# A retention layer's streamed weights: the second pair of a head's accumulating DMAs waits for the DMA transposes of the gated values

## The reference

```python
q, k, v, g = split(rms_norm(h) @ w_in)             # 8 heads: q, k 256 wide; v, g 512 wide
scores = einsum('bnihd,bnjhd->bnhij', rot(q), rot(k)) * decay
y = scores @ v  (+ the state that the first chunk hands to the second)
y = normalise each head of y
h = h + (silu(g) * y) @ w_out                      # the gated values
h = h + sigmoid(rms_norm(h) @ w_gate) * (p @ w_proj)
```

## Time and profile before

| | us |
|---|---|
| median of 3 executions | 1563.88 |
| lowest and highest of the 3 | 1559.8, 1565.68 |
| the profiled execution, its own time | 1568.04 |
| its span, first to last instruction | 1566.0 |
| TensorE busy | 1531.3 (98% of the span) |
| VectorE, ScalarE, GpSimd busy | 1124.6, 926.2, 28.8 |
| mean granted TensorE clock | 0.994 of full |

### The profile page before, as it was taken

One profiled execution on the slowest core, in us unless ns is written; L12 is line 12 of the kernel. 1 busy time (PEld: TensorE's weight loads), 2 busy tenths in 40 slices (PEclk: granted clock), 3 DMA queues, 4 the chain that ended last, 5 costly groups with the idle time before them and its releaser, 6 DMA issues.

```text
span 1566.0 us, 19940 instructions
## 1 busy us (share of the span) xinstructions
PE 1531.3 (98%) x6788; PEld 1261.6 (81%) x6788; DVE 1124.6 (72%) x1390; ACT 926.2 (59%) x1108; POOL 28.8 (2%) x40
## 2 busy tenths in 40 slices
PE   9988989999999999999999999999999999999997
PEld 7777868888788888888888888888888888888885
DVE  6968768797888888787767585685577557756665
ACT  7447554664747475575767656644664466446853
POOL 0000000000000000000000000000000000000000
PEclk9999999999999999999999999999999999999999
DMA  9496695977768596976565666755665576555651
GB/s 385 155 217 232 204 190 177 281 222 207 227 211 236 188 264 201 266 223 215 181 225 192 205 225 188 243 204 199 196 233 191 195 228 212 218 191 198 215 192 78
DMA packets 137529, 333.11 MB, mean 213 GB/s; under 512 B 80992, under 2 KB 81008, under 8 KB 116368
## 3 DMA queue, kind: packets, MB, share of 16 engines
q1 hardware_dynamic: 132608, 314.35, 60.5%
q0 software_dynamic: 4736, 17.95, 5.6%
q10 hardware_dynamic: 144, 0.26, 0.0%
HBM read 312.08 MB, written 2.10 MB: 201 GB/s over the span
## 4 chain that ended last, share of the span: by engine, by line
PE 80%; DMA 6%; ACT 4%; DVE 4%; SPq 4%; issue 2%; ACTq 0%; DVEq 0%
PE accA L512 9%; PE accA L514 9%; PE accA L513 9%; PE accC L512 9%; PE accC L514 9%; PE accC L513 9%; DMA w_raw<-in_stream_dram 6%; PE accB L512 6%; PE accB L514 5%; PE accB L513 5%; SPq L410 3%; ACT w_hi L871 2%; DVE w_lo L1251 1%; ACT words_e L950 1%; PE side L544 1%
## 5 line engine op out<-in xcount | busy, mean ns | idle before, releaser
L1321 DVE TENSOR_TENSOR w_lo<-w_raw,w_hi 128x1024 fp32r<-128x1024 f32 x326 | 396.0, 1224 | 226.1 <-ACT w_hi L858 224.4
L858 ACT CAST w_hi<-w_raw 128x1024 fp32r<-128x1024 f32 x326 | 341.0, 1055 | 268.8 <-PE accA L514 99.5
L871 ACT CAST w_hi<-w_raw 128x1024 fp32r<-128x1024 f32 (+1 forms) x280 | 274.7, 1010 | 233.6 <-DMA w_raw<-in_stream_dram 71.3
L1251 DVE TENSOR_TENSOR w_lo<-w_raw,w_hi 128x1024 fp32r<-128x1024 f32 (+1 forms) x280 | 320.7, 1168 | 110.6 <-ACT w_hi L871 110.6
L512 PE MATMUL accA<-w_hi,xa_hi 128*128 128x512 f32 x452 | 176.0, 389 | 0.6 <-DVE w_lo L1321 0.6
L512 PE MATMUL accC<-w_hi,xa_hi 128*128 128x512 f32 x396 | 157.0, 396 | 19.9 <-DVE w_lo L1251 19.8
L514 PE MATMUL accA<-w_hi,xa_lo 128*128 128x512 f32 x452 | 175.9, 389 | 0.0
L513 PE MATMUL accA<-w_lo,xa_hi 128*128 128x512 f32 x452 | 175.8, 389 | 0.0
L513 PE MATMUL accC<-w_lo,xa_hi 128*128 128x512 f32 x396 | 155.6, 393 | 0.0
L514 PE MATMUL accC<-w_hi,xa_lo 128*128 128x512 f32 x396 | 155.5, 393 | 0.0
L512 PEld LDWEIGHTS accC<-w_hi,xa_hi 128*128 128x128 f32 x396 | 75.2, 190 | 39.5 <-DVE w_lo L1251 24.0
(11 more groups left out here) (275 smaller groups left out, 2807.1 us busy)
## 6 DMA issues: line engine op xcount, KB each, us to landing
w_raw<-in_stream_dram SPq DMA_DIRECT2D x162, 1024.0 KB, 4.8
w_raw<-in_stream_dram SPq DMA_DIRECT2D x224, 512.0 KB, 5.7
w_raw<-in_stream_dram POOLq DMA_DIRECT2D x28, 512.0 KB, 8.3
h<-in_x_dram SPq DMA_DIRECT2D x4, 512.0 KB, 12.8
xT_raw<-in_xT_dram SPq DMA_DIRECT2D x3, 512.0 KB, 13.7
dec<-in_decay_dram POOLq DMA_DIRECT2D x1, 1024.0 KB, 9.1
fgain<-in_final_gain_dram POOLq DMA_DIRECT2D x1, 1024.0 KB, 6.0
out_dram<-emb SPq DMA_DIRECT2D x1, 1024.0 KB, 3.8
```

The costliest lines, as they stand in the source:

```text
L858: act.copy(w_hi[:, r % RING, :], w_raw[:, r // 2, (r % 2) * 1024:(r % 2 + 1) * 1024]).then_inc(hi_ready, 1)
L871: act.copy(dst, unit_raw(name)).then_inc(hi_ready, 1)
L1251: dve.tensor_tensor(w_lo[:, u % RING, 0:n], unit_raw(ORDER[u]), w_hi[:, u % RING, 0:n].bitcast(F32), ALU.subtract).then_inc(lo_ready, 1)
L1321: dve.tensor_tensor(w_lo[:, r % RING, :], w_raw[:, r // 2, (r % 2) * 1024:(r % 2 + 1) * 1024], w_hi[:, r % RING, :].bitcast(F32), ALU.subt ...
```

## The change

In GpSimd's program for a head, one wait is added between the first pair of accumulating DMAs and the second:

```diff
                 add_block(hd, base, "X1a", "X2", "M1a")
                 add_block(hd, base, "X1b", "X2", "M1b")
+                pool.wait_ge(halvesT_landed, (2 * hd - 1) * 16 * TT)
                 wait_head_landed(pool, hd, "X2a")
                 add_block(hd, base, "X2a", "X3", "M1b")
                 wait_head_landed(pool, hd, "X2b")
                 add_block(hd, base, "X2b", "X3", "M1b")
```

## The result

The changed kernel takes 1544.01 us (median of 4 runs, 1542.46 to 1545.35) against 1561.98 us for the kernel before (median of 4, 1559.8 to 1565.68). The ratio is 0.9882 with a 95% interval of 0.9858 to 0.9906: 1.2% faster. The profiled execution took 1545.35 us, 22.7 us less than that of before.

The account below looks back on a forecast made before the run. TensorE was taken to bound heads 3 to 6, with long DMA stalls added in heads 1 and 2. From 1568.0 us, 18.5 for those stalls and half a microsecond for heads 3 to 7 came off: 1549, range 1543 to 1559.

Parts of the forecast that it names:

- main mechanism: Accumulating DMAs and transposes in flight together delay C5's load in heads 1 and 2, so TensorE stands and its clock drops.
- signs named ahead: In the loop: heads 1 and 2 within 1 us of others, no TensorE wait above 2 us, no ScalarE idling before M7a, M7b.
- (2): Heads 1 and 2 lose their long stalls, 10.6 and 7.9 us, together 18.5 us; C5 in head 1 just in time.
- (3): Heads 3 to 7: freed transposes and earlier C5 remove at most TensorE's small waits, 3.5 us; half a microsecond counted.
- Rival E: Heads 3 to 7 lose their waits too, all heads run at TensorE's 88.2 us: 1543 us; chance 0.13.
- A: The forecast itself: the loop's long stalls go and no new ones come, 1544 to 1555 us; chance 0.60.
- (4): Held X2a at M7a's cast: lands early by 2.8 us there, 4.8 at TensorE; X2b has more room; cost 0.
- Rival B: Sums land too late for M7a in seven heads, so slower; 1591 us with the longest landing; chance 0.05.
- Rival C: No effect: something else in heads 1 and 2, such as a load backlog, slows them; 1563 to 1568 us; chance 0.10.
- Rival D: One long stall stays, or a new wait of about 1 us at M7a or M6 in every head; 1557; chance 0.12.

Follow-up runs that it names:

- second trace: The kernel before, unedited, profiled a second time to see whether the long stalls fall in the same heads; 1568.75 us in the profiled execution.
- late-sum run: The changed kernel with one more GpSimd wait ahead of X2a, until the low part of C5 is made; 1575.88 us, 1.0063 of before.

## Why the prediction was right, step by step

**The direction and the main mechanism** held: 1544 us against 1549 forecast, inside 1543 to 1559, 1.2% against 1.0%. The two long stalls are gone, the clock is full throughout the loop, the transposes of all heads land within 5.7 us of their issue, and the pair is issued 0.3 to 0.8 us after that. Two of the signs named ahead did not come: the stretch of head 1 is 3.5 us longer than the others and not within 1 us, and in five places ScalarE was idle ahead of the casts of M7a and M7b.

**From 1549 to 1544.** Against the profiled execution of before, 1568.04, the terms gave 18.5 + 0.5 = 19 us and the traces have 17.5 + 5.2 = 22.7, which makes 1545.3; the last 1.3 us is that the changed kernel's profiled execution lies above its median.

**(2), the long stalls,** was sized well for this trace: heads 1 and 2 went from 99.69 to 91.32 and from 96.91 to 87.74 us, 17.5 us against 18.5 forecast. The load of C5 in head 1 was issued at 106.0 and landed at 111.2 (104.6 and 110.3 forecast), but TensorE did not wait for C5: it began it at 113.7 without a gap. It stood 1.2 us in that head, about the 1 us forecast, for another unit, C6. ScalarE's cast of C6, at 116.82, came behind its work on the transposed halves, and TensorE started C6 at 119.17 (rows of ScalarE, then of TensorE):

```profile
113.16 2.58 ACT L951 COPY words_e<-halvesT_e 128x1024 uint16<-128x1024 uint16 x2
...
116.82 1.04 ACT L872 CAST w_hi<-w_raw 128x1024 fp32r<-128x1024 f32 x1
...
119.17 0.50 PE L513 MATMUL accC<-w_hi,xa_hi 128*128 128x512 f32 x1 [1.19 <-DVE w_lo L1252]
```

That this microsecond agreed is luck. What was wrong is the reading that the long stalls belong to heads 1 and 2. The second trace has them in 1 and 7, and over many runs heads 1 and 2 are worth 10 us and heads 3 to 7 another 8. So the total came out near the forecast partly by luck too: less in heads 1 and 2 than the 18.5 us, and more in the rest than nothing.

**(3) is the term that was mis-sized.** I counted half a microsecond for heads 3 to 7 and kept 3.5 us as the upper end. In the traces the four stretches of heads 3 to 6 went from 89.14 + 90.03 + 88.96 + 88.68 = 356.8 to 351.6 us, 5.2 us, or 1.3 a head, and the busy time of 88.2 that I took for the floor was not one: with every unit on time a head takes 87.8. The upper end was too low as well: the small waits of the earlier trace rows are 3.5 us, and 5.2 us went. Rival E described this outcome (1543), with 0.13; the result lies 1 us from it and 5 from A's value.

**(4), the cover of the late sum,** held in its result, no wait of TensorE at M7a or M7b, but its room was overstated. X2a landed 9.1 us after its issue in head 6 (8 taken) and transposes landed at 547.1, so 556.5, that is 15.2 us after the first transpose; I had 577.5 - 562.5 = 15.0. The moment by which it is needed I took from the schedule of before, 582.3 - 562.5 = 19.8 us. That schedule had C5 late. In the changed kernel ScalarE's cast of C6 starts 556.5 - 541.3 = 15.2 us after the first transpose instead of 579.3 - 562.5 = 16.8, so the room ends at about 19.8 - 1.6 = 18.2 and is 3.0 us, not 4.8. The late-sum run agrees: landed after 20.8, TensorE stood 2.15 us. It also shows that a microsecond too late costs more than one, with the clock. X2b was taken to have more room than X2a, 4.0 us for an issue 0.86 us behind. It landed 3.8 us behind X2a in each head, so it had hardly more room than X2a, and it is X2b for which ScalarE waited in four heads. Rival B was thus nearer than its working said.

**Rival C** is refuted by the result, and its backlog in heads 1 and 2 by the second trace. What was right in it is that a plain load has a part: that of C4. **Rival D** did not come: both stalls went, and the wait of 1.2 us is in one head and not in every one. In the chances, 0.79 for faster counts half of D and not "a good third", 0.60 + 0.13 + 0.06; nothing else hangs on it. **The profiled execution against the median:** I read its 4.2 us above the median as a stall that differs between executions. The second trace and the range of 15 us over 21 runs agree with that, while the changed kernel's four runs lie within 2.9 us.

**The step that was incomplete** is the cause itself. Accumulating DMAs and transposes are in flight together in every head of the kernel before, also in those without a long stall, so "in flight together" is not sufficient. What the nine slow heads have in common is that C4's load was issued 0.5 us ahead of the first transpose and X2b 0.0 to 2.3 us after it, and seven of the nine had a long stall. That C4's load has a part rests on the runs with later transposes and with C4 held: in the latter two heads of one execution became slow, and with the wait none. Why these three stop each other was not found out.

## What to carry to other kernels

When a head of a loop now and then takes several microseconds longer for the same work, list for each pass when every DMA was issued and landed, and take a second trace of the same kernel before believing which pass is special. A DMA that nobody needs for a while can be held with one wait on an idle queue until the transfers on the critical path have landed; work out how late it may land from the schedule as it will be after the change, since removing one delay moves the next deadline forward. The gain can be larger than the long stalls themselves (here 6.8 and 7.4 us of standing still, and 22.7 us between the two traces), because the clock and the small waits go too.

## What the hardware showed that was not expected

The same DMA transpose of 256 KB took very different times to land, by what was in flight with it: 2.7 to 2.8 us in heads 2 to 7 of the run with later transposes and held sums, where C4's load had landed or was within 0.3 us of it and C5's was issued 1.5 us behind the second transpose; 4.4 to 5.7 us beside C4's load in the changed kernel; 6.0 to 9.5 us with accumulating DMAs partly beside it, in the heads of the kernel before that are not among the nine; and 12.2 to 16.7 us in the seven worst heads, all but one transpose of 6.3 us, where X2b itself took 12.5 to 16.0 us.

TensorE's clock fell to half while it stood still in each of the seven gaps of 6.0 to 7.4 us, and stayed there for 6.8 us, once for 10.2. But a shorter gap can be enough, and its length alone does not decide. In the late-sum run the clock fell within 0.7 us of the end of the gap, for 3.4 us, in heads 4 to 7 (gaps of 2.1 to 2.5 us) and not in heads 1 to 3 (2.0 to 2.5 us). In head 1 of three other runs it fell after gaps of 4.3 us (C4 held), 2.7 (later transposes) and 1.8 (copies for the transposes), and in head 7 of the run with C4 held a gap of 3.2 us left it at full.
